# A delta rule in chunks of 128 tokens instead of 64, and x at another address

## The reference

```
def gated_delta_chunked(q, k, v, g, beta):
...
    L = GDN_CHUNK
...
    g = jnp.cumsum(chunks(g), axis=-1)
...
    decay = jnp.exp(jnp.where(incl, g[..., :, None] - g[..., None, :], -jnp.inf))
    kb = k * beta[..., None]
    a_mat = jnp.where(strict, jnp.einsum('bhcld,bhcmd->bhclm', kb, k) * decay, 0.0)
    rhs = jnp.concatenate([v * beta[..., None], kb * jnp.exp(g)[..., None]], axis=-1)
    sol = lax.linalg.triangular_solve(a_mat + jnp.eye(L, dtype=jnp.float32), rhs,
                                      left_side=True, lower=True)
    u, w = jnp.split(sol, [DV], axis=-1)
    qk = jnp.where(incl, jnp.einsum('bhcld,bhcmd->bhclm', q, k) * decay, 0.0)

    def step(state, inp):
        qc, kc, uc, wc, gc, ac = inp
        v_new = uc - jnp.einsum('bhld,bhdv->bhlv', wc, state)
        o = (jnp.einsum('bhld,bhdv->bhlv', qc * jnp.exp(gc)[..., None], state)
             + jnp.einsum('bhlm,bhmv->bhlv', ac, v_new))
        g_last = gc[..., -1:]
        state = (state * jnp.exp(g_last)[..., None]
                 + jnp.einsum('bhld,bhlv->bhdv', kc * jnp.exp(g_last - gc)[..., None], v_new))
        return state, o
```

## Time and profile before

| what | value |
|---|---|
| median of 3 runs | 6119.5 us (6066.75 to 6120.64) |
| profiled execution, time | 6114.06 us |
| its span, first to last instruction | 6112.3 us |
| mean granted TensorE clock | 0.896 |
| TensorE busy | 5516.5 us (90%) |
| VectorE busy | 2908.6 us (48%) |
| ScalarE busy | 1643.2 us (27%) |
| GpSimd busy | 654.5 us (11%) |

### The profile page before, as it was taken

How to read it: one execution, slowest core, us unless ns; L and a number is a source line. 1 busy time by engine, 2 the same in 40 slices (tenths; PEclk the granted TensorE clock), 3 DMA queues, 4 the chain that set the end, 5 groups by cost and what they waited for, 6 DMA issues and landing times. The chain is left out here.

```text
span 6112.3 us, 64132 instructions
## 1 busy us (share of the span) xinstructions
PE 5516.5 (90%) x24636; PEld 4337.6 (71%) x24636; DVE 2908.6 (48%) x5398; ACT 1643.2 (27%) x2474; POOL 654.5 (11%) x408
## 2 busy tenths in 40 slices
PE   7779899999999999788998998999888998899998
PEld 6227678888878887677873676788677864667787
DVE  3674458886024444744322355443654323355433
ACT  2203333333222222311212223332311212223322
POOL 0750002222410000011000002000011000002000
PEclk8679899999999999877787898999887897889999
DMA  2002023555555554100110121222100210212222
GB/s 90 1 28 97 32 101 127 174 175 173 182 194 194 194 193 167 59 1 1 59 64 23 59 66 57 84 94 93 62 1 1 76 55 14 76 49 83 83 93 73
DMA packets 230158, 526.64 MB, mean 86 GB/s; under 512 B 19425, under 2 KB 87265, under 8 KB 228577
## 3 DMA queue, kind: packets, MB, share of 16 engines
q1 hardware_dynamic: 229856, 522.56, 25.3%
HBM read 446.98 MB, written 75.50 MB: 85 GB/s over the span
## 5 line engine op out<-in xcount | busy, mean ns | idle before, releaser
L244 DVE TENSOR_TENSOR weight_low<-ring,weight_high 128x1024 fp32r<-128x1024 f32 x566 | 696.4, 1231 | 1510.4 <-ACT weight_high L234 1509.9
L234 ACT CAST weight_high<-ring 128x1024 fp32r<-128x1024 f32 x674 | 706.8, 1049 | 2183.6 <-PE banks L77 2160.1
L75 PE MATMUL banks<-x_high,weight_high 128*128 128x512 f32 x1872 | 756.1, 404 | 116.9 <-DVE x_low L293 50.7
L76 PE MATMUL banks<-x_low,weight_high 128*128 128x512 f32 x1872 | 750.8, 401 | 0.0
L77 PE MATMUL banks<-x_high,weight_low 128*128 128x512 f32 x1872 | 749.8, 401 | 0.0
L75 PEld LDWEIGHTS banks<-x_high,weight_high 128*128 128x128 f32 x1872 | 360.3, 192 | 209.4 <-issue 70.1
L244 POOL TENSOR_TENSOR weight_low<-ring,weight_high 128x1024 fp32r<-128x1024 f32 x108 | 263.8, 2444 | 1898.4 <-ACT weight_high L234 1898.4
L76 PEld LDWEIGHTS banks<-x_low,weight_high 128*128 128x128 f32 x1872 | 360.5, 193 | 85.9 <-issue 1.0
L77 PEld LDWEIGHTS banks<-x_high,weight_low 128*128 128x128 f32 x1872 | 359.5, 192 | 86.1
L75 PE MATMUL banks<-xn_high,weight_high 128*128 128x512 f32 x1024 | 410.6, 401 | 0.7 <-ACT hT L1295 0.7
L75 PE MATMUL banks<-act_high,weight_high 128*128 128x512 f32 x1024 | 399.4, 390 | 13.0 <-DVE act_low L1502 13.0
(11 more groups left out here) (522 smaller groups left out, 9671.8 us busy)
## 6 DMA issues: line engine op xcount, KB each, us to landing
ring<-in_peer_u SPq DMA_DIRECT2D x128, 512.0 KB, 3.5
ring<-in_peer_v SPq DMA_DIRECT2D x128, 512.0 KB, 3.3
acts<-dot_act SPq DMA_DIRECT2D x128, 256.0 KB, 2.0
gates<-gate_block SPq DMA_DIRECT2D x64, 512.0 KB, 5.9
activations<-acts SPq DMA_DIRECT2D x128, 256.0 KB, 3.7
gates_in<-gates SPq DMA_DIRECT2D x128, 256.0 KB, 3.9
ring<-in_w_up SPq DMA_DIRECT2D x64, 512.0 KB, 3.2
ring<-in_w_down SPq DMA_DIRECT2D x64, 512.0 KB, 3.2
```

The lines of the kernel that those rows point to most:

```text
L75: nc.tensor.matmul(out, w_high, x_high, start=start, stop=False)
L76: nc.tensor.matmul(out, w_high, x_low, start=False, stop=False)
L234: self.nc.scalar.copy(self.wH[:, g % 2, 0:kc * P], self.ring[:, g % SLOTS, 0:kc * P]).then_inc(self.high_made, 1)
L244: ops.tensor_tensor(self.wL[:, g % 2, 0:kc * P], self.ring[:, g % SLOTS, 0:kc * P], self.wH[:, g % 2, 0:kc * P].bitcast(F32), ALU.subtract ...
```

## The change

Chunks become whole token tiles of 128. The masks neg64 and strict64 go (neg128 is used, and AT isn't masked again, since each level's table holds the strict part); a seventh level is added to the table, and so one more level of four jobs to the doubling stage; the cumulative gates run over 128 tokens; the gates at the chunk ends are read from PSUM by the subtraction itself; the scan has four steps instead of eight, each with full 128-wide operands. In the scan vn now waits for the previous output product, and the last step leaves out state product, decay and sum. The table of constants shrinks from 1665 to 1537 floats (1568 rounded up), and an unused tensor of 96 floats, 384 bytes, is declared in front of x_high. Core of the diff:

```
-CONST = dict(neg128=(0, 128), neg64=(128, 128), strict64=(256, 128), level=(384, 768), causal=(1152, 512), inv_freq=(1664, 1))
-CONST_N = 1665
+LEVELS = 7
+CONST = dict(neg128=(0, 128), level=(128, 896), causal=(1024, 512), inv_freq=(1536, 1))
+CONST_N = 1537
...
         cumN = sb("cumN", [P, TT, P])
+        sb("x_offset", [P, 96])
         xH = sb("x_high", [P, DC, T], F32R)
...
-            for t in range(2 * TT):
-                s = slice(t * 64, (t + 1) * 64)
-                last = v.tensor_tensor_scan(cum[64:96, s], ones[64:96, 0:64], e[64:96, s], 0.0, ALU.mult, ALU.add)
+            for t in range(TT):
+                s = slice(t * P, (t + 1) * P)
+                last = v.tensor_tensor_scan(cum[64:96, s], ones[64:96, :], e[64:96, s], 0.0, ALU.mult, ALU.add)
...
-                        v.tensor_tensor(Dm[x % 2], Dm[x % 2], wide(cst("neg64")), ALU.add).then_inc(masked, 1)
-                        v.tensor_copy(g_last[:, x, :], banks[b].rearrange("p (c n) -> p c n", n=64)[:, :, 63:64].squeeze(2))
-                        t_ = tiles4(banks[b])
-                        v.tensor_copy(g_end[0:64, x, :], t_[0:64, :, 63:64].squeeze(2))
-                        link(v.tensor_copy(g_end[64:128, x, :], t_[64:128, :, 127:128].squeeze(2)))
-                        v.tensor_tensor(g_end[:, x, :], g_end[:, x, :], cumN[:, :, A_ROWS + h:A_ROWS + h + 1].squeeze(2), ALU.subtract)\
+                        v.tensor_tensor(Dm[x % 2], Dm[x % 2], wide(cst("neg128")), ALU.add).then_inc(masked, 1)
+                        chunk_ends = tiles4(banks[b])[:, :, P - 1:P].squeeze(2)
+                        v.tensor_copy(g_last[:, x, :], chunk_ends)
+                        v.tensor_tensor(g_end[:, x, :], chunk_ends, cumN[:, :, A_ROWS + h:A_ROWS + h + 1].squeeze(2), ALU.subtract)\
                             .then_inc(ends, 1)
...
-                        link(v.tensor_tensor(AT[:, x], AT[:, x], wide(cst("strict64")), ALU.mult))
...
-            jobs = [(k, x) for k in range(1, 6) for x in range(B4)]
+            jobs = [(k, x) for k in range(1, LEVELS) for x in range(B4)]
...
-                    for c in range(8):
-                        t, half = divmod(c, 2)
-                        r = slice(64 * half, 64 * half + 64)
-                        s = slice(64 * c, 64 * c + 64)
+                    for c in range(TT):
+                        s = slice(P * c, P * c + P)
                         pe.wait_ge(state_ready, c + 1)
                         for x in range(B4):
-                            last = nc.tensor.matmul(banks[0][r, x * P:(x + 1) * P], wT[:, x, s], S[:, x, :], start=True, stop=True)
+                            last = nc.tensor.matmul(banks[0][:, x * P:(x + 1) * P], wT[:, x, s], S[:, x, :], start=True, stop=True)
                         last.then_inc(ws_done, 1)
                         if c >= 1:
                             pe.wait_ge(o_copied, c)
                         for x in range(B4):
-                            nc.tensor.matmul(banks[4 + x][:, 0:64], S[:, x, :], qg[:, x, s], start=True, stop=False)
+                            nc.tensor.matmul(banks[4 + x][:, 0:P], S[:, x, :], qg[:, x, s], start=True, stop=False)
                         pe.wait_ge(v_new, c + 1)
+                        if c < TT - 1:
+                            for x in range(B4):
+                                last = nc.tensor.matmul(banks[2][:, x * P:(x + 1) * P], kd[:, x, c, :], vn[:, x, :], start=True, stop=True)
+                            last.then_inc(ds_done, 1)
                         for x in range(B4):
-                            last = nc.tensor.matmul(banks[2][:, x * P:(x + 1) * P], kd[r, x, t, :], vn[r, x, :], start=True, stop=True)
-                        last.then_inc(ds_done, 1)
-                        for x in range(B4):
-                            last = nc.tensor.matmul(banks[4 + x][:, 0:64], vn[r, x, :], acT[r, x, t, 64 * half:64 * half + 64],
-                                                    start=False, stop=True)
+                            last = nc.tensor.matmul(banks[4 + x][:, 0:P], vn[:, x, :], acT[:, x, c, :], start=False, stop=True)
                         last.then_inc(o_done, 1)
...
+                    for c in range(TT):
                         dve.wait_ge(ws_done, c + 1)
-                        v.tensor_tensor(vn[r], uN[r, :, t, :], banks[0][r, :].rearrange("p (x n) -> p x n", n=P), ALU.subtract)\
+                        if c:
+                            dve.wait_ge(o_done, c)
+                        v.tensor_tensor(vn[:], uN[:, :, c, :], banks[0].rearrange("p (x n) -> p x n", n=P), ALU.subtract)\
                             .then_inc(v_new, 1)
...
+                        if c < TT - 1:
+                            dve.wait_ge(state_ready, c + 1)
+                            v.tensor_tensor(Sd[:], S[:], g_last[:, :, c:c + 1].to_broadcast([P, B4, P]), ALU.mult).then_inc(decayed, 1)
+                            dve.wait_ge(decayed, c + 1)
+                            dve.wait_ge(ds_done, c + 1)
+                            v.tensor_tensor(S[:], Sd[:], banks[2].rearrange("p (x n) -> p x n", n=P), ALU.add).then_inc(state_ready, 1)
```

More of the change, by code:

```diff
@@ L2043, in delta_rule @@
         vn = sb("gdn_vn", [P, B4, P])
-        g_last = sb("gdn_last", [P, B4, 8])
+        g_last = sb("gdn_last", [P, 2 * B4, TT])[:, 0:B4]
         g_end = sb("gdn_end", [P, 2 * B4, TT])[:, 0:B4]
@@ L2185, in _ @@
                             last = nc.tensor.matmul(banks[2 + j % 2][:, s], Wb[j % 2][:, t, :], Tt[:, x, t, :], start=True, stop=True)
-                            if k < 5:
+                            if k < LEVELS - 1:
                                 last = nc.tensor.matmul(banks[4 + j % 2][:, s], Tt[:, x, t, :], Wb[j % 2][:, t, :], start=True, stop=True)
@@ L2262, in _ @@
                     v.memset(S[:], 0.0).then_inc(state_ready, 1)
[L2263 to L2266, removed]
+                    for c in range(TT):
                         dve.wait_ge(ws_done, c + 1)
-                        v.tensor_tensor(vn[r], uN[r, :, t, :], banks[0][r, :].rearrange("p (x n) -> p x n", n=P), ALU.subtract)\
+                        if c:
+                            dve.wait_ge(o_done, c)
+                        v.tensor_tensor(vn[:], uN[:, :, c, :], banks[0].rearrange("p (x n) -> p x n", n=P), ALU.subtract)\
                             .then_inc(v_new, 1)
-                        v.tensor_tensor(Sd[:], S[:], g_last[:, :, c:c + 1].to_broadcast([P, B4, P]), ALU.mult).then_inc(decayed, 1)
-                        dve.wait_ge(decayed, c + 1)
-                        dve.wait_ge(ds_done, c + 1)
-                        v.tensor_tensor(S[:], Sd[:], banks[2].rearrange("p (x n) -> p x n", n=P), ALU.add).then_inc(state_ready, 1)
-                        dve.wait_ge(state_ready, c + 2)
+                        if c < TT - 1:
[4 more added lines that the diff above has]
+                            v.tensor_tensor(S[:], Sd[:], banks[2].rearrange("p (x n) -> p x n", n=P), ALU.add).then_inc(state_ready, 1)
                 @block.scalar
                 def _(act):
-                    for c in range(8):
+                    for c in range(TT):
                         act.wait_ge(o_done, c + 1)
-                        nc.scalar.copy(xp[:, 8 + 4 * hb:12 + 4 * hb, 64 * c:64 * c + 64],
-                                       psum[:, 4:8, 0:64]).then_inc(o_copied, 1)
+                        nc.scalar.copy(xp[:, 8 + 4 * hb:12 + 4 * hb, P * c:P * c + P],
+                                       psum[:, 4:8, 0:P]).then_inc(o_copied, 1)
         rmsnorm(nc, "gdn_norm", lambda c: xp[:, 8 + c, 0:T], lambda c: yT[:, c, :], 8, 1, tools, P, lambda c: col("gdn_g"),
@@ L2459, in _layout_second @@
     neg = lambda keep: np.where(keep, 0.0, NEG)
-    levels = [((m ^ l) >= 1 << k) & ((m ^ l) < 2 << k) & (l > m) for k in range(6)]
+    levels = [((m ^ l) >= 1 << k) & ((m ^ l) < 2 << k) & (l > m) for k in range(LEVELS)]
     inv = 10000.0 ** (-np.arange(0, 64, 2, dtype=np.float32) / np.float32(64))
-    parts = dict(neg128=neg(l >= m), neg64=neg((l >= m) & (l // 64 == m // 64)), strict64=(l > m) & (l // 64 == m // 64),
-                 level=np.concatenate(levels, axis=1), causal=np.concatenate([np.zeros((P, 384)), neg(l <= m)], axis=1),
+    parts = dict(neg128=neg(l >= m), level=np.concatenate(levels, axis=1), causal=np.concatenate([np.zeros((P, 384)), neg(l <= m)], axis=1),
                  inv_freq=np.tile(inv, 4)[:, None])
```

## The result

| | before | after |
|---|---|---|
| median of the runs, us (four each) | 6116.2 (6066.75 to 6120.64) | 5938.6 (5937.55 to 5941.38) |
| profiled execution, us | 6114.06 | 5938.35 |
| its span, us; mean granted clock | 6112.3; 0.896 | 5936.4; 0.911 |

The ratio is 0.9728, with a 95% interval of 0.9678 to 0.9778. The profiled executions lie 175.7 us apart, where 168.5 were forecast. The spread is a result too: the runs of before lie 54 us apart, those of after 4.

A forecast was written before the change was run, and what follows sets the result against it. TensorE's queue, or chains it waits for, was taken as the bound. Scans -143.5, doubling +42.9, first stage -17.4, cumulative sums -0.5, address -50 sum to -168.5: 6114.06 becomes 5945.6, predicted as 5947 us, range 5930 to 5998.

The forecast's parts named there:

- Scans: Delta rule's scans over chunks: eight steps become four of 3.8 us, 15.6 us a scan at 2.4 GHz; -143.5 us in all.
- two terms of the chain: Within a scan step's chain of 3.82 us: each waiting matrix group at 1.06 us, the first group and the state product.
- The low start: Scans beginning at 1.2 GHz before the clock rises: 1.7 us lost in each of three scans of four.
- The two covers: In the scan, vn's wait for the previous output product adds nothing; TensorE's wait for ScalarE's copy is covered by under 0.1 us.
- Clock: New scans run at 2.4 GHz like the doubling stage's same-shaped products; rival, scans stay at 1.2 GHz: 5995 us, chance 0.07.
- one run with two high scans more: Among the old kernel's runs, 6066.75 us is 53 us lower, as two more scans at full clock would make it.
- Doubling: Doubling stage: one more level, 16 more TensorE-bound jobs of 2.68 us, all on the path; +42.9 us.
- First stage: First stage, VectorE's chain per head: strict mask and two copies go, 1.09 us for 16 heads, period 5.4; -17.4 us.
- TensorE's products stayed hidden: First stage: products for the head after next take 4.65 us, hidden in the 5.4 us period with 0.7 to spare.
- Address: Second block's 512-column products with x: 8100 at 6.2 ns less, -50 us; rival, address does nothing: 5997 us, chance 0.11.
- the starting address as the only thing left: First and second block streams, alike otherwise, start 1325 and 1287 products in 300 us; the start address is taken as cause.
- a whole number of 512: x_high moves from 36,992 to 36,864 bytes after weight_high, a multiple of 512 like the first block's operands, giving the faster spacing.

The follow-up runs named there:

- experiment 1: The changed kernel without the unused 384 bytes in front of x, so x_high starts 128 bytes past a multiple of 512 from weight_high; 5994.1 us.
- experiment 10: The changed kernel with ScalarE's two exponentials of the first stage in the other order; 5939.2 us, beside 5937.4 for the changed kernel on the same chip.
- experiment 8: The changed kernel with two vn buffers in turn, so vn waits for the output product before the last; 5936.1 us.
- experiment 6: The kernel before with both output products of the scan over all 128 columns of the token tile, chunks still 64; 6056.3 us, ratio 0.997.
- experiment 7: The kernel before with both output products and the first product (state and w) over the whole token tile; 6046.5 us, ratio 0.994.
- B: The kernel before the change; median 6116.2 us beside the changed kernel, and 6063.5, 6114.0 and 6071.3 us in groups of experiment runs.
- experiment 2: The kernel before with only the 384 bytes added in front of x, old chunks, masks and doublings kept; 5977.8 us, ratio 0.987.
- experiment 3: The changed kernel with 128 unused bytes in front of weight_high, moving weights and operands of both blocks together; 5936.2 us, ratio 0.980.

## Why the prediction was right

**Scans.** The step was forecast at 3.8 and took 3.95 us, a scan at full clock 16.1 for 15.6. The error lies in two terms of the chain: a group that has been waiting takes 1.16 us (2733.30 and 2735.24), not the 1.06 of one that follows another (2734.30 and 2736.24). That is 0.20 in a step; 0.07 of it came back, since the first hand-over took 0.03 and not 0.10. The low start cost 1.48 us (5.43 less 3.95) for 1.7. That three of the four scans began low, as forecast, is luck: in experiments 1 and 10 two did, and with x at 64 bytes one. The two covers held: vn starts 1.19 us into a step, when the previous output product is long done (2736.24 + 1.06 = 2737.30, 0.05 into the next step, as forecast), and ScalarE's copy ends at 2737.92, 0.67 into a step whose second group starts 1.00 into it (2734.30 behind 2733.30). Experiment 8 confirms the first of them.

**Clock.** Taking the nearest row by shape, the doubling stage, and not the old scan, was the choice that the forecast rested on. It held, and experiments 6 and 7 bear it out. The Trainium skill, page "TensorE: Matmul & The Clock Gate", Part 1, has activity release the throttle. The trace agrees for products of the full shape, where the clock was at 1.00 from the second step of the first scan on, and differs for the half ones: busy for 58.0 of 59.1 us at 0.52. The prediction counts three low scans of four, and one run with two high scans more, but not how far this count can go: it is one execution's. B's runs went from 6035 to 6126, a width of 90 us, where the clock of four scans would make 102. So roughly 77 of the 176 us are the clock of three scans, three times 25.6, and against B's best runs the change is worth about 98 us (6036 to 5938), 1.6%. The table agrees: with all old scans at 33.41 us the scans bring 133.6 - 68.9 = 64.7 in place of 141.7, and all rows together 99. That the new products are what brought the 77 us is shown only in part: a low start costs them little, but in experiment 2 the old products had the high clock too.

**Doubling.** The job's price of 2.68 us and its count were right: 42.9. The 2.8 us above it are clock, as two of the four stages stand at 12 us more instead of 10.7 (0.94 against 0.96).

**First stage.** The period came out at 5.39 for 5.4 us, which makes 17.6 over 16 heads for the forecast 17.4, and TensorE's products stayed hidden. The other 10.5 us were not foreseen, the largest miss in the sum. They lie at the starts: from the first gather, which spreads the row of gates, to VectorE's first subtraction it is 3.14 us now (2606.05 to 2609.19) and was 5.79 before:

```profile
2608.33 1.11 PE L1755 MATMUL banks<-cum,ident 32*128 32x512 f32 x1 [1.93 <-PEq L40]
...
2614.12 0.69 DVE L2077 TENSOR_TENSOR ring<-banks,cumN 128x512 f32<-128x512 f32 x1 [6.99 <-PE banks L2067]
```

The pause ahead is 1.93 us in both; behind it the granted clock is 0.51 up to the subtraction before, and 1.00 after. The four starts are alike within 0.3 us in either kernel; together they make 10.4. That doesn't come from the new products: in experiment 2, whose first stages are the old ones, two starts took 3.15 us and two 5.83, and without the offset (experiment 1) two of the changed kernel's took 5.7, one 4.75 and one 3.15. The prediction had no term for the clock at these starts.

**Address.** 8304 products by 6.0 ns are 50 us; the groups give 3 x (11.9 + 2.9 + 3 x 0.7) = 50.7 for those three operand kinds beside the earlier trace rows, the offset alone about 47, its removal 49.8. The step that took the starting address as the only thing left was right in its result; of its form, the distance from the weights held (experiment 3), and a whole number of 512 was too narrow, as 256 bytes do as well. The Trainium skill, page "SBUF — State Buffer", section "Operand start alignment", asks for a multiple of the element's size only, and says that this is about legality, not speed. Every distance here fulfils it, and the spacing differs all the same, from 226.7 to 232.6 ns.

The time itself, 5938.6 for 5947, comes closer than the terms do: the first stage's 10.5 us are partly offset by the doubling's 2.8 and the scans' 1.8 the other way.

Why the distance should matter is not shown by any run, nor is what sets the moment at which the clock falls.

## What to carry to other kernels

Cut a busy TensorE's time by stage and set the granted clock beside it: a stage that is 98% busy at 0.52 has a factor near two hidden in it, and here it lost little of that once its products had the full shape. Where two gapless streams of the same products start a different number in the same time, look at the distance of the operands' starts, which a dummy tensor can change. And where one program's runs lie 1.5% apart, take its profile as one draw, and compare with its best runs too.

## What the runs showed of the hardware

- TensorE, fully queued with products of 64 rows or columns, stayed at 1.2 GHz for almost the whole of a 59 us scan (0.52), and in another scan of the same execution ran at 2.4 GHz (33.4 us). With products of 128 columns in two of four groups the clock rose about 19 us into the two scans that began low (8 us lost); with three of four the one low start lost 1.6 us, with full products three lost 1.5 each.
- Products of 512 columns (L75 to L77) follow each other every 226.7 ns or every 232.6 at a clock of 1.00, by the distance of their right-hand operand from the weights: 0 and 256 bytes past a multiple of 512 give 226.7, 64 gives 229 and 128 gives 232.6. Moving all operands together changes nothing.
- A 128x128x128 group of eight instructions took 1.16 us behind a wait and 1.06 in a queue.
- A first stage that starts behind a pause of 1.93 us took 3.14 us to VectorE's first subtraction at a clock of 1.00 and 5.79 at 0.51.
